# One layer's attention outputs turned and multiplied as they become ready, half of a conditioning vector computed later, and rows made by turning broadcast columns

## The chip, the cores and the metric

The program runs on 1 core of one Trainium2 chip. The metric is the device time in microseconds (us) of one execution. Each engine (PE the matrix engine, DVE, ACT, POOL, and SP, which issues most loads) works through its own list in order and meets the others at semaphores.

## The reference, cut to what matters

Two transformer blocks of depth 2 each, 256 positions of 1024 channels, all in f32. The change touches the first block:

```python
for layer in range(DEPTH):
    mod = c @ w_ada[layer] + b_ada[layer]
    sh_a, sc_a, g_a, sh_f, sc_f, g_f = [m[:, None, :] for m in jnp.split(mod, 6, -1)]
    h = x * (1.0 + sc_a) + sh_a
    u = h @ w_in[layer]
    ...
    mix = jnp.concatenate([y_ret, y_ssd, y_swa], -1) @ w_out[layer]
    x = _layer_norm(DEEPNORM_ALPHA * x + (1.0 + g_a) * mix, ln_g[layer, 0], ln_b[layer, 0])
    h = x * (1.0 + sc_f) + sh_f
    if layer % 2 == 0: f = _swiglu(h, ffn_w_gate[i], ffn_w_up[i], ffn_w_down[i])
    else:              f = _moe(h, router_w[i], router_b[i], ...)
    x = _layer_norm(DEEPNORM_ALPHA * x + (1.0 + g_f) * f, ln_g[layer, 1], ln_b[layer, 1])
```

`y_ret` (retention) has 256 columns, `y_ssd` 512 and `y_swa` (windowed attention) 256. The second block (mLSTM, convolution, cross-attention, FFN) is not touched.

## The kernel before, in words

**Weights.** Every weight matrix is streamed from HBM in chunks of 1 MB in the order of `stream_plan`. SP loads a chunk into a slot of RAW (two slots in the first mixer, four from the FFN on), ACT rounds it to HI (`split_hi`, line 430), DVE subtracts to get LO (`split_lo`, line 439), and PE makes each product from three matmuls (lines 444 to 446). A slot is free again after LO; HI and LO have three places each, free again when PE is done with the chunk.

**The conditioning vector.** `c @ w_ada` is not done on PE: DVE multiplies each 128-row piece of `w_ada` by a column of `c` and adds it to a sum (`ada_step`, lines 694 and 697), SP loads the pieces (`ada_load`, line 684), and at the end PE adds over the partitions with one-column matmuls (`pe_ada_sum`, line 725). The 12288 results of both layers are computed in blocks of 2048. In the first mixer, 32 pieces of 512 KB pass through two half slots of RAW: blocks 1 and 2 of layer 0. Block 2 holds the scale and the output gate (`g_f`) of the FFN. The 24 pieces of layer 1, 1 MB each, pass during the FFN (line 697 too), through two slots in AR.

**The end of a mixer** (`pe_mixer1`, `act_mixer1`, `dve_mixer1`, called for l = 0 and l = 1). DVE finishes retention (a norm over each head, lines 1453 to 1478), gates the SSD output in two halves (1467, 1470; each half waits for 8 or 16 matmuls of `y`, lines 1138 and 1140), and scales the attention output (1481). ACT squares the gated SSD output (1276), POOL takes the root, DVE applies it (1488). Then the 1024 mixed columns in R are turned (128x128 transposes on PE, line 544), rounded by ACT (572) and DVE (582, 584), and multiplied by the four chunks of `w_out` (c0 to c3 below): c0, c1, then c2 and c3 as a pair, bank by bank. All four chunks start only after all four turns have been issued. After each of the last pair's four banks DVE adds the residual and takes statistics (929, 931, 934), normalises (942), and PE turns X for the FFN or the router.

**Rows.** A vector that lies as columns (8 columns of 128) and is needed as a row in all partitions is made by DVE multiplying the identity by each column (`dve_diag`, line 894, 8 instructions) and PE multiplying ones by the result (`pe_rows`, line 901, 8 matmuls, two passes each). ACT copies it (907). This is done six times: (0,0), (0,1), (1,0), scale, shift and gate.

**What sets the order.** Everything is written out by hand. `sp_stream` issues chunk i, then the `ada_load`s that the table `SIDE_AFTER` or the FFN position names; each `ada_load` waits for the DVE step that frees its slot, and all later loads stand behind it on SP. `ada()` in `dve_mixer1` is a pair of `ada_step`s and stands between the `split_lo`s.

```python
SIDE_AFTER = {..., 13: (8,), 14: (9,), 15: (10, 11, 12), 16: (13, 14, 15)}
...
if i == (moe_first if l else CH["out0"][3] + 1):
    s.wait_ge(*dve_fm(("mix", l), "lo", 3))
    sp_gains(s, l, 0)
```

Chunks 13 to 16 are c0 to c3 of layer 0; 17 and 18 are the FFN's first gate and up chunks. In layer 1, after the last pair, PE multiplies early keys (`pe_keys`, line 1636), ACT issues eight small loads (`act_small`, lines 2275 and 2277) and copies the keys (1646), and only then PE turns X for the router (544).

## Time and profile before

| | |
|---|---|
| median of 3 runs | 2753.8 us (2753.72 to 2757.09) |
| the profiled execution, its span | 2756.4 us |
| PE busy in it | 2655.7 us (96%) |
| DVE busy in it | 2194.9 us (80%) |
| first mixer, FFN, second mixer end at about | 207, 429, 568 us |

The page names busy time of each engine, the granted clock of PE in 40 slices, the chain of waits that ended last and the costliest groups. Since PE is busy nearly all the time, what counts is where it is idle or at its lower clock: the timelines of single engines say that. One profiled execution is shown; it lies 2.6 us above the median.

### The profile page before, as it was taken

To read this page: it belongs to the slowest core of one execution; us is meant where nothing else is said; L and a number is where in the kernel's file an instruction comes from. 1 tells how busy PE (TensorE), PEld (TensorE's weight loads), DVE (VectorE), ACT (ScalarE), POOL (GpSimd) and SP (SyncE) were. 2 spreads that over 40 slices of the span, in tenths; PEclk is the share of its full clock that TensorE was granted. 3 is DMA by queue.
4 is the path that set the end of the run, shared out by engine and by line. 5 is a ranking of instruction groups with operands and counts; after the bars stand their busy time and mean duration, and the time that the engine had idled before them with its cause. 6 is when DMAs were issued, how large, how long until landed. Compare 5 with 4: busy or idle time off the path is not lost.

```text
span 2756.4 us, 37885 instructions
## 1 busy us (share of the span) xinstructions
PE 2655.7 (96%) x15712; PEld 2358.6 (86%) x15712; DVE 2194.9 (80%) x2513; ACT 1519.4 (55%) x1567; POOL 47.4 (2%) x83
## 2 busy tenths in 40 slices
PE   6969999989999999999999999999999999999998
PEld 5859998878888888888888889999899999998898
DVE  6967677778888888888888879885487788954777
ACT  3514335547677677777777754544554564444554
POOL 2000000000000000000000000000000000000000
PEclk9979999989999999999999999999999998999999
DMA  8649865369999999999999952354455533444453
GB/s 312 235 162 336 312 240 168 120 212 378 351 350 353 345 359 349 360 348 358 348 359 346 364 184 87 135 183 173 157 184 184 186 125 130 154 153 168 153 184 115
DMA packets 376065, 669.86 MB, mean 243 GB/s; under 512 B 26825, under 2 KB 199503, under 8 KB 371023
## 3 DMA queue, kind: packets, MB, share of 16 engines
q1 hardware_dynamic: 358400, 662.55, 68.2%
...
## 4 chain that ended last, share of the span: by engine, by line
PE 88%; DVE 7%; ACT 2%; DMA 1%; issue 1%; POOL 0%; ACTq 0%; SPq 0%; DVEq 0%; POOLq 0%
PE PS L444 25%; PE PS L446 24%; PE PS L445 24%; PE PS L544 2%; PE PS L2477 2%; DVE LO L439 2%; PE PS L1636 2%; DVE AR L2767 1%; PE PS L1871 1%; PE PS L1908 1%; PE PS L2363 1%; DMA RAW<-in_w_ada_dram 1%; ACT HI L430 1%; DVE AR L697 1%; PE PS L2354 1%
## 5 line engine op out<-in xcount | busy, mean ns | idle before, releaser
L439 DVE TENSOR_TENSOR LO<-RAW,HI 128x2048 fp32r<-128x2048 f32 x410 | 930.2, 2273 | 231.5 <-ACT HI L430 231.3
L430 ACT ACTIVATE HI<-RAW 128x2048 fp32r<-128x2048 f32 x410 | 780.0, 1903 | 346.3 <-PE PS L446 292.9
L444 PE MATMUL PS<-X1H,HI 128*128 128x256 f32 (+1 forms) x2128 | 611.4, 287 | 6.2 <-DVE X1L L584 4.2
L445 PE MATMUL PS<-X1L,HI 128*128 128x256 f32 (+1 forms) x2128 | 605.5, 285 | 0.0
L446 PE MATMUL PS<-X1H,LO 128*128 128x256 f32 (+1 forms) x2128 | 605.2, 284 | 0.0
L444 PE MATMUL PS<-HI,X1H 128*128 128x512 f32 x1056 | 431.6, 409 | 0.9 <-DVE LO L439 0.4
L444 PEld LDWEIGHTS PS<-X1H,HI 128*128 128x128 f32 (+1 forms) x2128 | 409.4, 192 | 11.1 <-issue 8.5
L446 PE MATMUL PS<-HI,X1L 128*128 128x512 f32 x1056 | 413.7, 392 | 0.0
L445 PE MATMUL PS<-LO,X1H 128*128 128x512 f32 x1056 | 413.0, 391 | 0.0
L445 PEld LDWEIGHTS PS<-X1L,HI 128*128 128x128 f32 (+1 forms) x2128 | 409.6, 192 | 2.0
L446 PEld LDWEIGHTS PS<-X1H,LO 128*128 128x128 f32 (+1 forms) x2128 | 409.3, 192 | 0.8
L439 DVE TENSOR_TENSOR LO<-AR,HI 128x2048 fp32r<-128x2048 f32 (+1 forms) x147 | 334.8, 2278 | 58.6 <-ACT HI L430 57.7
L430 ACT ACTIVATE HI<-AR 128x2048 fp32r<-128x2048 f32 (+1 forms) x147 | 280.2, 1907 | 121.3 <-PE PS L446 117.0
L444 PE MATMUL PS<-HI,X2H 128*128 128x512 f32 x840 | 333.9, 398 | 3.3 <-DVE LO L439 3.3
L445 PE MATMUL PS<-LO,X2H 128*128 128x512 f32 x840 | 330.8, 394 | 0.0
L446 PE MATMUL PS<-HI,X2L 128*128 128x512 f32 x840 | 330.5, 393 | 0.0
L444 PEld LDWEIGHTS PS<-HI,X1H 128*128 128x128 f32 x1056 | 199.2, 189 | 48.3 <-issue 8.5
L445 PEld LDWEIGHTS PS<-LO,X1H 128*128 128x128 f32 x1056 | 199.4, 189 | 45.5 <-issue 6.7
L446 PEld LDWEIGHTS PS<-HI,X1L 128*128 128x128 f32 x1056 | 198.8, 188 | 42.9
L2767 DVE SCALAR_TENSOR_TENSOR AR<-AR,PC 128x256 f32<-128x256 f32 x480 | 193.9, 477 | 0.1
L444 PEld LDWEIGHTS PS<-HI,X2H 128*128 128x128 f32 x840 | 160.4, 191 | 35.7 <-DVE LO L439 3.7
L446 PEld LDWEIGHTS PS<-HI,X2L 128*128 128x128 f32 x840 | 159.8, 190 | 34.1
...
## 6 DMA issues: line engine op xcount, KB each, us to landing
...
```

Source lines behind the costliest of these rows:

```text
L430: a.activation(HI[:, n % NH, 0:size(i)], raw_at(i), ACT.Copy).then_inc(*hi.up(i))
L439: v.tensor_tensor(LO[:, m % NH, 0:n], raw_at(i), HI[:, m % NH, 0:n].bitcast(F32), ALU.subtract).then_inc(*lo.up(i))
L444: t.matmul(o, lh, rh, start=first, stop=False)
L445: t.matmul(o, lh, rl, start=False, stop=False)
L446: return t.matmul(o, ll, rh, start=False, stop=last)
L544: z = t.transpose(d, s_, ident[0:n, 0:n])
L697: v.scalar_tensor_tensor(o, slot, pcol("c", k), o, ALU.mult, ALU.add).then_inc(*dve_ada.up("step", m))
L1636: z = t.matmul(PS[:, bank, 256 * nb:256 * nb + 256], w[:, c, 128 * nb:128 * nb + 128], cols[:, c, :], start=(c == 0), stop=(c == 7))
L1871: z = t.matmul(PS[:, gather_bank(x, half), 128 * c:128 * c + 128], HM[:, k, 512 * half + 128 * c:512 * half + 128 * c + 128], PP[:, x % 2, ...
L1908: t.matmul(PS[:, scatter_bank(x, q), :], PGT[:, x % 2, 128 * k:128 * k + 128], YE[:, x % 2, ns], start=True, stop=True).then_inc(*pe_moe.u ...
L2477: z = t.matmul(PS[:, b, 256 * k:256 * k + 256], MF[:, c, 128 * k:128 * k + 128], w[:, c, :], start=(c == 0), stop=(c == 7))
L2767: v.scalar_tensor_tensor(UC[:, c, :], UP[:, c, k:k + 256], pcol(f"cv_dw_w{l}", 8 * k + c), UC[:, c, :], ALU.mult, ALU.add).then_inc(*dve_t ...
```

## The change

1. **Mixed columns.** Their order in R becomes attention, retention, SSD, SSD, and the chunks of `w_out` are loaded in that order. PE turns the attention columns after the first half of `y`, the retention columns after the second, multiplies the first chunk, then turns the SSD columns, multiplies the second chunk and then the pair. ACT and DVE follow the same order; ACT squares each SSD half apart.
2. **Conditioning.** Block 2 of layer 0 keeps only its first 1024 results (8 pieces of 512 KB in place of 16). The other half, `g_f`, becomes sum 6: 4 more pieces of 1 MB (two row blocks of 1024 columns each) in the FFN, at the unit numbers n = 8, 17, 26 and 27 that had no piece. PE sums it right after sum 5.
3. **Rows.** `dve_diag` is gone. `pe_rows` turns each column, read 128 times over by a step of zero: 8 transposes.
4. **SP.** No `ada_load` stands behind c3 any more, two fewer stand ahead of it, and the two loads of gains move behind the FFN's first two chunks.

```diff
-        out += u_tm(A["w_out"][l], 0, 8, f"out{l}")
+        out += u_tm(A["w_out"][l], 6, 8, f"out{l}") + u_tm(A["w_out"][l], 0, 6, f"out{l}")
...
+    ADA, ADA_OF, ADA_SUM = [], {}, ((0, 0, 16), (0, 16, 16), (0, 32, 8), (1, 0, 16), (1, 16, 16), (1, 32, 16), (0, 40, 8))
+    STAGE = ([ar(8192 + 2048 * i, 2048) for i in range(4)], [RAW[:, 2, 0:1024], RAW[:, 2, 1024:2048]],
+             [ar(8192, 2048), ar(10240, 2048)])
+    SUMMED = (ar(2304, 2048), RAW[:, 3, :], RAW[:, 3, 0:1024], ar(12288, 2048), ar(14336, 2048), ar(12288, 2048),
+              ar(5120, 1024))
...
+        for k in range(8):
+            step(2, 1, ((k, 0, 1024),))
+        for n in (3, 4, 5):
             for k in range(8):
...
+                step(n, 2, ((k, 0, 2048),))
+            for k in ((0,), (2,), (4, 6))[n - 3]:
+                step(6, 2, ((k, 0, 1024), (k + 1, 0, 1024)))
...
-        for j in range(16):
-            z = t.matmul(PS[:, bank, j:j + 1], acc[:, 128 * j:128 * j + 128], ones[:, 0:1], start=True, stop=True)
+        for j in range(ADA_SUM[n][2]):
+            z = t.matmul(PS[:, bank, at + j:at + j + 1], SUMMED[n][:, 128 * j:128 * j + 128], ones[:, 0:1], start=True,
+                         stop=True)
...
-    DG = ar(5120, 8, 128)
-
-    def dve_diag(v, tag, cols):
-        for c in range(8):
-            z = v.tensor_scalar(DG[:, c, :], ident, cols[:, c:c + 1], None, ALU.mult)
-        z.then_inc(*dve_res.up("diag", tag))
-
-    def pe_rows(t, tag):
-        t.wait_ge(*dve_res("diag", tag))
+    def pe_rows(t, tag, cols, bank=0):
+
         for h in range(2):
-            for c in range(4):
-                z = t.matmul(PS[:, h, 128 * c:128 * c + 128], ones, DG[:, 4 * h + c, :], start=True, stop=True)
-            z.then_inc(*pe_res.up("rows", tag, h))
-
-    def act_rows(a, tag, dst):
+            turn(t, [(PS[:, bank + h, 128 * c:128 * c + 128], view(cols[:, 4 * h + c:4 * h + c + 1], [0, 128]))
+                     for c in range(4)]).then_inc(*pe_res.up("rows", tag, h))
+
+    def act_rows(a, tag, dst, bank=0):
         for h in range(2):
             a.wait_ge(*pe_res("rows", tag, h))
-            a.activation(dst[:, 512 * h:512 * h + 512], PS[:, h, :], ACT.Copy).then_inc(*act_res.up("rows", tag, h))
+            a.activation(dst[:, 512 * h:512 * h + 512], PS[:, bank + h, :], ACT.Copy).then_inc(*act_res.up("rows", tag, h))
...
-        t.wait_ge(*act_ev(f"in{l}r2", 1))
-        pe_rows(t, (l, 0))
-        t.wait_ge(*dve_mix("gate", l, 1))
-        for k in range(2):
+        def turn_mix(cp):
+            t.wait_ge(*dve_mix(("swa", "retout", "ssd", "ssd")[cp], l))
+            turn(t, [(PS[:, MIX_BANKS[cp], 256 * ci + 128 * tt:256 * ci + 128 * tt + 128],
+                      R[:, tt, 128 * (2 * cp + ci):128 * (2 * cp + ci) + 128])
+                     for ci in range(2) for tt in range(2)]).then_inc(*pe_fm.up(("mix", l), cp))
+
+        def y(k):
             for h in range(8):
                 xv = lambda j: XD[:, j, 64 * h:64 * h + 64]
                 o = PS[:, 4 + k, 64 * h:64 * h + 64]
...
                 if k:
                     z = t.matmul(o, E8[:, h, 256:384], xv(1), start=False, stop=True)
             z.then_inc(*pe_mix.up("y", l, k))
+
+        def out_rows(n):
+            i = CH[f"out{l}"][n]
+            t.wait_ge(*lo(i))
+            t.wait_ge(*dve_fm(("mix", l), "lo", n))
+            mm_down(t, i, lambda c: X2H[:, 2 * n + c, :], lambda c: X2L[:, 2 * n + c, :], [4, 5, 6, 7], n == 0,
+                    False).then_inc(*used.up(i))
+
+        t.wait_ge(*act_ev(f"in{l}r2", 1))
+        t.wait_ge(*dve_ada("mod", 4 if l else 1))
+        pe_rows(t, (l, 0), MOD[:, l, 16:24])
+        t.wait_ge(*dve_mix("gate", l, 1))
+        y(0)
+        turn_mix(0)
+        y(1)
+        turn_mix(1)
+        t.wait_ge(*dve_mix("gated", l, 1))
+        t.wait_ge(*act_mix("qt", l, 1))
+        out_rows(0)
         t.wait_ge(*act_res("rows", (l, 0), 1))
-        pe_to_fm(t, ("mix", l), R, [2, 3, 0, 1], order=MIXED,
-                 ready=lambda cp: dve_mix("retout", l) if cp == 0 else dve_mix("swa", l) if cp == 3 else dve_mix("ssd", l))
-        def between(j):
-            if l == 1 and j == 1:
-                t.wait_ge(*dve_fm(("mix", 1), "lo", 3))
-                pe_rows(t, "scale")
-            if l == 1 and j == 2:
-                t.wait_ge(*act_res("rows", "scale", 1))
-                pe_rows(t, "shift")
-            if l == 1 and j == 3:
-                t.wait_ge(*act_res("rows", "shift", 1))
-                pe_rows(t, "gate")
-
-        pe_gemm_tm(t, f"out{l}", X2H, X2L, [4, 5, 6, 7], lambda j: dve_fm(("mix", l), "lo", j), between)
-        if l == 0:
-            pe_ada_sum(t, 2, 1)
+        turn_mix(2)
+        turn_mix(3)
+        if l == 1:
+            t.wait_ge(*dve_fm(("mix", 1), "lo", 1))
+            t.wait_ge(*dve_res("combined", 1, 0))
+            pe_rows(t, "scale", HSC, 2)
+        out_rows(1)
+        if l == 1:
+            t.wait_ge(*dve_fm(("mix", 1), "lo", 3))
+            pe_rows(t, "shift", HSH)
+            t.wait_ge(*act_res("rows", "shift", 1))
+            t.wait_ge(*dve_ada("mod", 5))
+            pe_rows(t, "gate", MOD[:, 1, 40:48])
+        else:
+            pe_ada_sum(t, 2, 2)
+        pair = CH[f"out{l}"][2:]
+        for n in range(2):
+            t.wait_ge(*lo(pair[n]))
+            t.wait_ge(*dve_fm(("mix", l), "lo", 2 + n))
+        mm_down_pair(t, pair, lambda n, c: X2H[:, 4 + 2 * n + c, :], lambda n, c: X2L[:, 4 + 2 * n + c, :], [4, 5, 6, 7],
+                     f"out{l}").then_inc(*used.up(pair[1]))
...
-        for k in range(2):
+
+        def squares(k):
             a.wait_ge(*dve_mix("gated", l, k))
             for g in range(2):
                 z = a.activation(SQR[:, k, 256 * g:256 * g + 256], XS[:, k, 256 * g:256 * g + 256], ACT.Square,
                                  scale=1.0 / 16, accum_out=m4[:, 2 * k + g:2 * k + g + 1])
-        z.then_inc(*act_mix.up("ssdvar", l))
-        act_fm_scaled(a, ("mix", l), [2, 3, 0, 1], X2H, lambda c: pcol(f"ssd_norm{l}", c - 2) if 2 <= c < 6 else None, MIXED)
+            z.then_inc(*act_mix.up("ssdvar", l, k))
+
+        mixed = lambda *cps: act_fm_scaled(a, ("mix", l), MIX_BANKS, X2H, lambda c: pcol(f"ssd_norm{l}", c - 4) if c > 3 else None,
+                                           cps)
+        mixed(0)
+        squares(0)
+        mixed(1)
+        squares(1)
+        mixed(2, 3)
+        if l == 1:
+            act_rows(a, "scale", SCR, 2)
         split_hi(a)
         if l == 1:
-            act_rows(a, "scale", SCR)
             act_memory_cols(a, "router", 0, raw[slot_of[CH["mf"][0]]](CH["mf"][0]), raw_cols(CH["mf"][0]))
+            act_rows(a, "shift", SHR)
+            act_rows(a, "gate", GB2)
+        split_hi(a)
         split_hi(a)
         if l == 1:
-            act_rows(a, "shift", SHR)
-        split_hi(a)
-        if l == 1:
-            act_rows(a, "gate", GB2)
             act_small(a)
...
+        if l == 1:
+            dve_combine(v, 1, 0)
         gate(0)
         gate(1)
-        v.wait_ge(*pe_mix("pt", l, 3))
-        dve_diag(v, (l, 0), MOD[:, l, 16:24])
-        ada()
...
-        v.wait_ge(*dve_mix("skip", l))
-        for k in range(2):
+
+        def gated(k):
...
-        v.wait_ge(*act_mix("rg", l))
+
+        mixed = lambda *cps: dve_fm_scaled(v, ("mix", l), MIX_BANKS, X2H, X2L,
+                                           lambda c: pcol(f"ssd_norm{l}", c - 4) if c > 3 else None, cps)
         v.wait_ge(*pe_mix("pv", l))
         v.wait_ge(*dve_mix("den", l))
-        R4 = R[:, :, 768:1024].rearrange("p t (h d) -> p t h d", h=4)
+        v.tensor_tensor(R[:, :, 0:256].rearrange("p t (h d) -> p t h d", h=4),
+                        PS[:, 7, :].rearrange("p (t h d) -> p t h d", t=2, h=4), view(den, [4, 2], [1, 4], [0, 64]),
+                        ALU.mult).then_inc(*dve_mix.up("swa", l))
+        v.wait_ge(*dve_mix("skip", l))
+        gated(0)
+        v.wait_ge(*act_mix("rg", l))
         v.wait_ge(*pool_rs("ret", l))
         v.tensor_tensor(O8, O8, every8(v8), ALU.mult).then_inc(*dve_mix.up())
         v.wait_ge(*dve_mix.last())
-        v.tensor_tensor(R[:, :, 0:256], R[:, :, 768:1024], O8.rearrange("p (t h) d -> p t (h d)", t=2),
+        v.tensor_tensor(R[:, :, 256:512], R[:, :, 768:1024], O8.rearrange("p (t h) d -> p t (h d)", t=2),
                         ALU.mult).then_inc(*dve_mix.up("retout", l))
-        v.wait_ge(*dve_mix.last())
-        v.tensor_tensor(R4, PS[:, 7, :].rearrange("p (t h d) -> p t h d", t=2, h=4), view(den, [4, 2], [1, 4], [0, 64]),
-                        ALU.mult).then_inc(*dve_mix.up("swa", l))
-        if l == 0:
-            ada()
-        else:
-            split_lo(v)
+        mixed(0)
+        gated(1)
+        mixed(1)
+        split_lo(v)
+        v.wait_ge(*dve_mix("retout", l))
         v.wait_ge(*pool_rs("ssd", l))
-        v.tensor_tensor(R[:, :, 256:768].rearrange("p t (g d) -> p t g d", g=2),
+        v.tensor_tensor(R[:, :, 512:1024].rearrange("p t (g d) -> p t g d", g=2),
                         XS.rearrange("p t (g d) -> p t g d", g=2), view(m4, [2, 2], [1, 2], [0, 256]),
                         ALU.mult).then_inc(*dve_mix.up("ssd", l))
-        dve_fm_scaled(v, ("mix", l), [2, 3, 0, 1], X2H, X2L, lambda c: pcol(f"ssd_norm{l}", c - 2) if 2 <= c < 6 else None,
-                      MIXED)
-        if l == 1:
-            dve_combine(v, 1, 0)
-            v.wait_ge(*dve_res("combined", 1, 0))
-            dve_diag(v, "scale", HSC)
-        if l == 0:
-            split_lo(v)
         ada()
-        split_lo(v)
-        if l == 1:
-            v.wait_ge(*pe_res("rows", "scale", 1))
-            dve_diag(v, "shift", HSH)
+        mixed(2, 3)
+        split_lo(v)
         ada()
         split_lo(v)
-        if l == 1:
-            v.wait_ge(*pe_res("rows", "shift", 1))
-            dve_diag(v, "gate", MOD[:, 1, 40:48])
-        ada()
-        split_lo(v)
-        ada()
+        split_lo(v)
 
         def last_sum():
             if l == 0:
-                dve_ada_sum(v, 2, 1)
+                dve_ada_sum(v, 2, 2)
                 v.wait_ge(*dve_ada("mod", 2))
                 dve_combine(v, 0, 0)
...
             if n in (9, 18, 28):
                 t.wait_ge(*dve_ffn("ffn", "hid", p - 1))
                 pe_ada_sum(t, 2 + n // 9, 2 * ((p + 1) % 2))
+            if n == 28:
+                pe_ada_sum(t, 6, 2 * ((p + 1) % 2), 16)
...
-            t.wait_ge(*dve_ada("mod", 5))
+            t.wait_ge(*dve_ada("mod", 6))
...
-            pe_rows(t, (0, 1))
+            pe_rows(t, (0, 1), MOD[:, 0, 40:48])
...
-            if n < 27 and n not in (8, 17, 26):
-                ada_step(v, ada_of(n))
+            if n < 28:
+                ada_step(v, ADA1 + n)
...
+        dve_ada_sum(v, 6, 2, 16)
         dve_ada_sum(v, 5, 2)
-        dve_diag(v, (0, 1), MOD[:, 0, 40:48])
         dve_combine(v, 0, 1)
...
-            g.wait_ge(*act_mix("ssdvar", l))
+            g.wait_ge(*act_mix("ssdvar", l, 1))
...
     SIDE_AFTER = {1: (0,), 4: (1,), 5: (2,), 6: (3,), 8: (4,), 10: (5,), 11: (6,), 12: (7,), 13: (8,), 14: (9,),
-                  15: (10, 11, 12), 16: (13, 14, 15)}
+                  15: (10, 11)}
...
-                if i == (moe_first if l else CH["out0"][3] + 1):
+                if i == (moe_first if l else CH["out0"][3] + 3):
                     s.wait_ge(*dve_fm(("mix", l), "lo", 3))
                     sp_gains(s, l, 0)
...
-            if 0 <= n < 24 and n not in (8, 17):
-                ada_load(s, ada_of(n) + 2)
+            if 0 <= n < 26:
+                ada_load(s, ADA1 + n + 2)
```

On SP, behind c2 of layer 0 (first row), before:

```order
L419 DMA RAW<-in_w_out_dram 128x2x1024
L684 DMA RAW<-in_w_ada_dram 128x1024 x6
L419 DMA RAW<-in_w_out_dram 128x2x1024
L684 DMA RAW<-in_w_ada_dram 128x1024 x6
L916 DMA AR<-in_ln_g_dram 128x1024
L916 DMA AR<-in_ln_b_dram 128x1024
L419 DMA RAW<-in_ffn_w_gate_dram 128x8x256
```

and now:

```order
L419 DMA RAW<-in_w_out_dram 128x2x1024
L705 DMA RAW<-in_w_ada_dram 128x1024 x4
L419 DMA RAW<-in_w_out_dram 128x2x1024
L419 DMA RAW<-in_ffn_w_gate_dram 128x8x256
L419 DMA RAW<-in_ffn_w_up_dram 128x8x256
L933 DMA AR<-in_ln_g_dram 128x1024
L933 DMA AR<-in_ln_b_dram 128x1024
```

Ahead of c3 stand 4 pieces in place of 6, and none between c3 and the FFN's first chunk in place of 6 and the gains.

On DVE, layer 0, from the last turned SSD columns (line 584) to the residual (line 929, now 946), before:

```order
L584 SCALAR_TENSOR_TENSOR X2L<-PS,PC,X2H 128x256
L439 TENSOR_TENSOR LO<-RAW,HI 128x2048 [waits hi]
L697 SCALAR_TENSOR_TENSOR RAW<-RAW,PC 128x1024 [waits dve_ada,ada4]
L697 SCALAR_TENSOR_TENSOR RAW<-RAW,PC 128x1024 [waits dve_ada,ada5]
L439 TENSOR_TENSOR LO<-RAW,HI 128x2048 [waits hi]
L697 SCALAR_TENSOR_TENSOR RAW<-RAW,PC 128x1024 [waits dve_ada,ada4]
L697 SCALAR_TENSOR_TENSOR RAW<-RAW,PC 128x1024 [waits dve_ada,ada5]
L439 TENSOR_TENSOR LO<-RAW,HI 128x2048 [waits hi]
L697 SCALAR_TENSOR_TENSOR RAW<-RAW,PC 128x1024 [waits dve_ada,ada4]
L697 SCALAR_TENSOR_TENSOR RAW<-RAW,PC 128x1024 [waits dve_ada,ada5]
L439 TENSOR_TENSOR LO<-RAW,HI 128x2048 [waits hi]
L697 SCALAR_TENSOR_TENSOR RAW<-RAW,PC 128x1024 [waits dve_ada,ada4]
```

and now:

```order
L584 SCALAR_TENSOR_TENSOR X2L<-PS,PC,X2H 128x256
L439 TENSOR_TENSOR LO<-RAW,HI 128x2048 [waits hi]
L721 SCALAR_TENSOR_TENSOR RAW<-RAW,PC 128x1024 [waits dve_ada,ada4]
L721 SCALAR_TENSOR_TENSOR RAW<-RAW,PC 128x1024 [waits dve_ada,ada5]
L439 TENSOR_TENSOR LO<-RAW,HI 128x2048 [waits hi] x2
L946 TENSOR_TENSOR AR<-PS,AR 128x512 [waits pe_tm,act_res]
```

Four pairs of conditioning steps (the last row begins the fourth) stood between those columns and the residual; one is left. The LO of c1, once the first of four, now stands ahead of the SSD columns.

## Rows read from the trace of the kernel before

**Rows 1.** Page, part 1: busy us (share of the span) x instructions

```profile
PE 2655.7 (96%) x15712; PEld 2358.6 (86%) x15712; DVE 2194.9 (80%) x2513; ACT 1519.4 (55%) x1567; POOL 47.4 (2%) x83
```

**Rows 2.** Stretches: length, busy us (x) of five engines, PEclk, DMA share, GB/s

```profile
149.00:159.20 10.20, 7.01 (x24) 5.96 (x25) 9.38 (x15) 3.43 (x11) 1.44 (x2) 0.50 0.31 103
...
176.40:186.60 10.20, 8.19 (x36) 6.42 (x35) 0.00 (x0) 0.00 (x0) 0.00 (x0) 1.00 0.98 308
186.60:213.90 27.30, 12.90 (x58) 12.07 (x59) 21.52 (x36) 8.49 (x11) 1.62 (x4) 0.50 0.46 155
213.90:271.90 58.00, 56.88 (x432) 54.79 (x431) 45.09 (x27) 23.05 (x18) 0.00 (x0) 1.00 0.89 328
...
398.20:401.60 3.40, 3.40 (x19) 3.40 (x18) 2.97 (x15) 0.00 (x0) 0.00 (x0) 0.50 0.48 141
...
435.70:531.30 95.60, 92.43 (x645) 83.41 (x643) 73.71 (x132) 53.10 (x81) 2.72 (x5) 1.00 0.39 131
```

**Rows 3.** Chain of waits, 130 to 215 us: start, us, what

```profile
169.41 4.35 DMA RAW<-in_w_ada_dram
...
176.41 12.19 DMA RAW<-in_ffn_w_gate_dram
...
201.60 0.60 DVE AR L929
```

**Rows 4.** Timeline of SP: start, us from first to last issue

```profile
133.04 20.25 SPq L684 DMA_DIRECT2D RAW<-in_w_ada_dram  x6
160.11 0.38 SPq L419 DMA_DIRECT2D RAW<-in_w_out_dram  x1
161.30 14.12 SPq L684 DMA_DIRECT2D RAW<-in_w_ada_dram  x6
```

**Rows 5.** Timelines of DVE and ACT, first mixer's end [idle before <-releaser]

```profile
136.22 1.65 DVE L894 TENSOR_SCALAR AR<-CST,MOD 128x128 f32<-128x128 f32 x8
...
150.47 2.47 DVE L697 SCALAR_TENSOR_TENSOR RAW<-RAW,PC 128x1024 f32<-128x1024 f32 x2
```

```profile
165.04 1.92 ACT L430 ACTIVATE HI<-RAW 128x2048 fp32r<-128x2048 f32 x1 [8.06 <-DMA RAW<-in_w_out_dram]
```

**Rows 6.** Timeline of PE, first mixer's end and FFN start

```profile
138.02 3.04 PE L901 MATMUL PS<-AR,CST 128*128 128x128 f32 x16 [1.38 <-DVE AR L894]
...
149.97 1.94 PE L544 MATMUL PS<-CST,AR 128*128 128x128 f32 x8 [3.00 <-DVE AR L1478]
...
171.84 0.47 PE L444 MATMUL PS<-HI,X2H 128*128 128x512 f32 x1 [3.28 <-DVE LO L439]
...
211.79 0.56 PE L444 MATMUL PS<-X1H,HI 128*128 128x256 f32 x1
```

**Rows 7.** Chain of waits, 100 to 620 us: the FFN's end

```profile
394.16 3.47 PE PS L725 x32
...
410.44 0.87 PE PS L544 x8
411.32 1.79 PE PS L901 x16
```

**Rows 8.** DVE in the FFN: its timeline, then its conditioning steps grouped

```profile
390.45 2.29 DVE L439 TENSOR_TENSOR LO<-RAW,HI 128x2048 fp32r<-128x2048 f32 x1 [1.32 <-ACT HI L430]
392.66 0.68 DVE L1716 TENSOR_TENSOR AR<-AR,PS 128x512 f32<-128x512 f32 x1
```

```profile
L697 DVE SCALAR_TENSOR_TENSOR AR<-AR,PC 128x2048 f32<-128x2048 f32 x21 | 49.3, 2346 | 0.0
```

**Rows 9.** Timelines of ACT and PE, second mixer's end

```profile
564.86 0.40 ACTq L2275 DMA_DIRECT2D BT<-in_ml_w_gate_dram  x1
...
572.79 0.60 ACT L1646 ACTIVATE AR<-PS 128x512 f32<-128x512 f32 x1 [7.34 <-issue]
```

```profile
562.87 1.95 PE L901 MATMUL PS<-AR,CST 128*128 128x128 f32 x16
...
573.49 1.94 PE L544 MATMUL PS<-CST,X 128*128 128x128 f32 x16 [1.76 <-issue]
```

82 lines of the change are left out of this document (44 added, 38 removed).

## The prediction

> **What bounds the kernel now.** I read the page first. PE is busy 96% of the span and DVE 80% [rows 1], so time can only come out where PE is idle, runs at its lower clock, or does work that goes away. The second view is the granted clock by stretches [rows 2]: from 149.0 to 159.2 us and from 186.6 to 213.9 us it was 0.50 (1.2 GHz), in the long stretches 1.00 (2.4 GHz). The weak spot is the passage from the first mixer to the FFN. The stretch from 176.4 shows PE busy for 8.2 us, so the last pair of output products ended at 184.6; the FFN's first product started at 211.8 [rows 6]. These 27 us hold only a sum and the turns of X. The third view, the chain of waits, says what filled them [rows 3]: a conditioning piece under way for 4.35 us, then the FFN's first weight chunk for 12.2 us from 176.4, and DVE takes the last of the four banks of the residual at 201.6 although PE had finished it at 184.6. DVE's list has four conditioning pairs and the LO of that chunk ahead of the residual, and SP's list has the pieces ahead of the chunk.
>
> The same queue makes PE late earlier. SP spent 20.25 us on six pieces before c3 could be issued at 160.1, and 14.1 us on the six behind it [rows 4]; ACT got c3 at 165.0 [rows 5], and PE waited 3.3 us and started the pair at 171.8 [rows 6]. Before that PE waited 1.4 us for the diagonals and 3.0 us for the retention columns [rows 6]. Slices of a second kind stand at the second mixer's end [rows 9]: ACT issues eight small loads from 564.9 to 572.8, and PE, though done with the keys at 571.7, turns X only at 573.5.
>
> **The change, layer 0.** I lay the new order out with the durations of this trace.
> - Diagonals: DVE's 1.65 us at 136.2 goes [rows 5], as does the conditioning pair behind it (2.5 us and its wait). Retention, which began at 141.25, begins at 136.2. PE's rows cost 1.79 us as matmuls at the full clock [rows 7]; eight turns cost 0.87 us [rows 7]. The trace has no turn of a column read by a step of zero. Bounds: 0.87 us as any turn, 1.79 us if it went like the matmuls that it replaces. I take 0.87, the same instruction. PE had finished its previous work at 136.6 and goes on without the 1.4 us wait.
> - Rows 0.9, half of `y` 1.8, a turn, second half 3.6 us: `y` ends at 144.1 (was 147.0). DVE gates it (1.5 us after a short latency) by 145.8. c0, rounded at 132.5, then starts at 145.9 in place of 155.75 and takes 5.5 us, to 151.4. During it ACT squares, POOL takes the root (some 1.5 us) and DVE applies it by 150.2. The SSD turns and c1 follow to 157.8; c1's LO now comes at 148.7.
> - SP: the pieces behind c2 wait for the DVE pair that now runs from 150.2 to 152.7 (2.5 us [rows 5]). c3 goes out at 153.2, not 160.1 [rows 4]. It landed 4.9 us after its issue [rows 4, 5]; with a piece beside it I allow 5.4. HI 1.9 us [rows 5], then LO 2.3 us [rows 8] behind the last conditioning pair: ready at 163.0, against 171.6.
> - The sum over 8 columns of block 2, not 16, fits between 159.2 and 161.1, ahead of the pair. Three more conditioning pairs are no longer between PE and the residual. The FFN's first chunk leaves when c2's LO is done, at 156.7, lands at about 162.5, and its LO is done at 166.8, when the pair's first bank is done too. Nothing on DVE stands ahead of the residual after that.
> - The pair took 12.75 us (171.84 to 184.6) with a piece of slow clock; I keep that: 163.0 + 12.75 = 175.7. From the last bank to the FFN's first product it was 211.8 - 201.6 = 10.2 us [rows 3, 6]. New start: 185.9. **Term 1: 211.8 - 185.9 = -25.9 us.** Bounds: -22 if c0 falls to the low clock and c3 lands 2 us later; -29 if the pair runs at the full clock throughout (11.2 us) and the turns of X too.
>
> **The FFN.** It takes in 4 pieces of 1 MB, 4 steps of DVE (two halves of 1.28, so 2.5 us each) and 16 one-column passes on PE. The first two steps fall where DVE waits for HI; PE, busy 56.9 of the first 58.0 us [rows 2] and without a wait from there to unit 28, shows the cover; 21 grouped steps of DVE waited 0.0 us for data [rows 8], with the DMA engines at 0.89 in the first 58 us [rows 2]. I cost those at nothing; if that cover is gone, a step costs 2.5 us, or a chunk 2.8 us (328 GB/s at a share of 0.89 is 369 at full share). The last two fall at units 26 and 27. There DVE had one wait of 1.32 us [rows 8], then the hidden product at 392.66, and PE's sum started at 394.2 behind it. Adding 5.0 and taking off the wait moves that product to 396.3, and its end to 396.9: PE waits 2.8 us. Sum 6 is half of sum 5's 3.5 to 3.7 us [rows 7]: +1.8. Behind a sum the clock was 0.50 for 3.4 us [rows 2]; with 5 us more of little work I add one such stretch, 1.7 us lost. The rows (0,1) give back 0.9. The memory rows wait for the last step, now at about 396 in place of 387, and are needed at 408: free. **Term 2: +2.8 + 1.8 + 1.7 - 0.9 = +5.4 us** (bounds +1 and +10).
>
> **Layer 1.** There are no pieces here; DVE loses its four diagonals. `y` ends at 527.4 in place of 528.0, c0 starts at 529.1 in place of 536.6, because the SSD norm is no longer ahead of it. Then 5.5 for c0, 0.9 for two turns, 0.9 for scale, 5.5 for c1, 0.9 for shift, a new wait of some 1.6 us (gate goes to the banks that ACT must first have read, and ACT has 3.3 us of memory columns ahead of that), 0.9 for gate, 11.2 for the pair: its end is 556.5, against 562.9 [rows 9]. What counts is behind it: ACT's last HI waits for the pair's first chunk (about 555.0), ends at 556.9, and only then ACT issues its loads, 7.9 us (564.86 to 572.79 [rows 9]). The keys are copied at 565, PE turns X at 565.6 and not 573.5 [rows 9]. The new wait is hidden as long as it stays under 1 us more. **Term 3: -7.9 us** (bounds -6 and -9).
>
> Sum: -25.9 + 5.4 - 7.9 = **-28.4 us**, so a span of 2728.0 in place of 2756.4. That execution lay 2.6 us above the median of the three runs, which the sum leaves alone: **2725.4 us**.
>
> A rule that speaks against the change. Rows of turns here did not lower the clock: 435.7 to 531.3 is at 1.00 throughout [rows 2], and turns of four and eight in a row lie in it. The Trainium skill (TensorE: Matmul & The Clock Gate, Part 4: PE-mode transpose) says that the full clock does not engage for transposes, since they do not count as PE being busy in the same way. By that rule, the six sets of rows that were matmuls would each invite a stretch at 0.50; that is rival D.
>
> **The rivals.** All against 2753.8.
> - **A, the late chunk stays late.** c3 is still behind two pieces of conditioning, each waiting for a DVE step, and the FFN's second chunk behind c3's LO. If ACT, squaring in two parts between roundings, holds up the SSD norm by some 6 us and DMA is shared between c3, a piece and the FFN's chunk, the pair starts at 170 and the residual gains only the time after it. Half of term 1 is left, 13 us: -13 + 5.4 - 7.9 = -15.5, **2738**. For it: each load landed late wherever several were under way (12.2 us [rows 3]). Against: four such loads were, now two are.
> - **B, the FFN takes the extra pieces free.** DVE catches up before unit 26, and no further slow stretch comes: term 2 is +1, the sum -33, **2721**. For it: DVE's share in the FFN's later stretches is near 0.7. Against: units 26 and 27 come directly before the sum.
> - **C, the FFN becomes bound by SP and DMA: slower than before.** The gaps at n = 8 and 17 let the loads catch up; without them each unit needs two chunks of 1 MB, 5.7 us at 369 GB/s, and PE takes about 5.8 us for a unit (48 products 0.12 us apart). If each landing came 1.4 us late, 28 units would cost 39 us: -25.9 - 7.9 + 39 = +5, **2759**. It decides from 1.2 us a unit. Against: the DMA share was 0.89 [rows 2] and DVE never waited for a piece [rows 8] after the first.
> - **D, turns lower the clock.** Six sets of rows; a slow stretch of 3.4 us [rows 2] costs 1.7 us, and two in a row behind each would cost 3.4: +10 to +20, **2740**. Rows 2 speak against it.
> - **E, the change does nothing for the end of the mixer,** because something I don't see (the root on POOL, an order of semaphores) holds the residual: only terms 2 and 3, about -2, **2751**.
>
> **How the numbers follow.** Chances: forecast 0.63, A 0.13, B 0.11, C 0.03, D 0.06, E 0.04. The forecast's own range is 2719 to 2733 from the bounds. For 8 in 10 I go from 2715 (B with term 1 at its upper bound) to 2740 (A and D). A measurement of this kernel can tell 0.2%, 5.5 us, from no change. Faster by over 0.2%: the forecast, A, B and D, 0.93; within 0.2%: E, 0.04; slower: C, 0.03.
>
> **What would show it.** In the profile after: c0 of layer 0 starts near 146 and the pair near 163 us; SP issues c3 near 153; the FFN's first product starts near 186; no wait of PE for the FFN's first chunk. Sums 5 and 6 stand together near 371 with a PE wait of 2 to 3 us ahead. Rows take 0.9 us a set. In layer 1 the pair ends 26 to 27 us earlier than 562.9, counting terms 1 and 2, and X is turned 28 us earlier than 573.5; from there on both traces run in parallel. The forecast is wrong if the pair starts after 167, if the FFN from its first product to the last bank grows by over 10 us (it was 212), or if later parts differ by over 3 us.

## The result, and the profile after

| | before | after |
|---|---|---|
| median of all runs of this comparison | 2753.8 us (4 runs) | 2731.15 us (4 runs, 2726.36 to 2732.28) |
| ratio, 95% interval | | 0.9912 [0.9899, 0.9925] |
| the profiled execution, its span | 2756.4 us | 2730.0 us |
| PE's mean granted clock in it | 0.973 | 0.979 |

The changed kernel is faster by 0.9%. The median fell by 22.6 us where 28.4 were forecast; the spans of the two profiled executions lie 26.4 us apart. Two executions at a far lower clock, one of `cond_back2` (3769.6 us) and one of `both` (4887.9 us), are left out of every number below. The table of the three terms, read from the two traces:

| term | forecast | in the traces |
|---|---|---|
| 1, up to the FFN's first product | -25.9 | 211.79 to 189.90: -21.9 |
| 2, from there to the FFN's last bank | +5.4 | 212.3 to 218.0: +5.8 |
| 3, from there to the turning of X for the router | -7.9 | 149.4 to 139.2: -10.2 |
| sum | -28.4 | -26.4 |

From the router on both run in parallel: the spans differ by the 26.4 us that they differed by at the turning of X.

The page's busy line hardly moves against [rows 1]; PE is busy 12 us less, DVE 9:

```profile
PE 2643.8 (97%) x15664; PEld 2346.4 (86%) x15664; DVE 2186.1 (80%) x2466; ACT 1519.5 (56%) x1567; POOL 50.8 (2%) x83
```

**The first mixer's end.** The timeline of PE of the changed kernel, from the rows on (one line for each stretch that counts; start, busy us, what it did, and in brackets the idle time ahead and who ended it):

```profile
137.10 1.04 PE L544 MATMUL PS<-CST,MOD 128*128 128x128 f32 x8
137.98 1.90 PE L1158 MATMUL PS<-AR 128*128 128x64 f32 x16
140.28 0.66 PE L544 MATMUL PS<-CST,AR 128*128 128x128 f32 x4 [0.40 <-DVE AR L1527]
...
144.29 0.61 PE L544 MATMUL PS<-CST,AR 128*128 128x128 f32 x4
...
160.55 3.58 PE L749 MATMUL PS<-CST,RAW 128*128 128x1 f32 x16 [2.42 <-DVE RAW L721]
166.97 0.76 PE L444 MATMUL PS<-HI,X2H 128*128 128x512 f32 x1 [2.84 <-DVE LO L439]
...
188.07 2.18 PE L544 MATMUL PS<-CST,X 128*128 128x128 f32 x8 [1.75 <-DVE X1L L602]
189.90 0.56 PE L444 MATMUL PS<-X1H,HI 128*128 128x256 f32 x1
```

Of the two waits ahead of the rows and of the turned columns [rows 6] the first is gone and of the second 0.4 us are left, and a set of rows takes 1.04 us where the matmuls took 3.04 at the same place, mostly at the low clock (1.79 at the full one [rows 7]). c0 started at 146.03. PE then has nothing to do between c1 and the pair but the sum: it waits 2.4 and 2.8 us. The last line that answers to [rows 6] is the FFN's first product, at 189.90 for 211.79.

Why the pair starts at 167.0 and not at 163.0 stands in the timelines of SP and ACT and in the chain of waits of the same stretch:

```profile
133.17 21.16 SPq L705 DMA_DIRECT2D RAW<-in_w_ada_dram  x4
154.38 0.43 SPq L419 DMA_DIRECT2D RAW<-in_w_out_dram  x1
157.78 0.38 SPq L419 DMA_DIRECT2D RAW<-in_ffn_w_gate_dram  x1
```

```profile
162.47 1.91 ACT L430 ACTIVATE HI<-RAW 128x2048 fp32r<-128x2048 f32 x1 [8.64 <-DMA RAW<-in_w_out_dram]
165.26 1.91 ACT L430 ACTIVATE HI<-RAW 128x2048 fp32r<-128x2048 f32 x1 [0.88 <-DMA RAW<-in_ffn_w_gate_dram]
```

```profile
147.02 1.93 POOL SM L618
149.02 1.06 POOL SM L620
...
151.31 1.29 DVE RAW L721
152.70 1.29 DVE RAW L721
154.01 0.33 SPq L705
154.38 8.07 DMA RAW<-in_w_out_dram
162.47 1.92 ACT HI L430
164.42 2.30 DVE LO L439
```

The chain is the forecast's, link for link: POOL's root, the SSD norm on DVE, the conditioning pair, SP, c3. Two links were longer. POOL took 3.0 us for the root where I allowed 1.5, so SP issued c3 at 154.4, not 153.2; and c3, issued right behind the last two pieces, landed after 8.07 us, not 5.4.

Why the root took longer stands in the timelines of POOL and DVE. Its first operation in the kernel before, then DVE's LO of c1 in the changed kernel:

```profile
149.53 0.39 POOL L618 TENSOR_SCALAR SM<-SM 128x4 f32<-128x4 f32 x1 [2.91 <-ACT AR L1276]
```

```profile
146.56 2.28 DVE L439 TENSOR_TENSOR LO<-RAW,HI 128x2048 fp32r<-128x2048 f32 x1
```

In the changed kernel POOL's operation (147.02 in the chain) begins while that LO is under way and ends at 148.94, 0.1 us behind the LO's end at 148.84. So it is in both SSD norms of all fourteen traces of this case: the operation ends 0.1 us behind the DVE instruction that was under way when it began, be that a short product (0.39 us; before, `rows_only` and `order_back`), a conditioning step (1.06 us) or an LO (1.92 to 2.07 us). The new order has put c1's LO beside the root. No run moved it away, so what that would give is not shown.

c3 had company on both sides. The stretches from the last two pieces to c3's landing (columns as in [rows 2], the last is GB/s):

```profile
153.00:157.00 4.00, 4.00 (x19) 3.31 (x18) 4.00 (x6) 0.83 (x3) 0.00 (x0) 1.00 0.75 214
157.00:162.40 5.40, 2.98 (x15) 2.45 (x13) 3.23 (x3) 0.00 (x0) 0.00 (x0) 0.80 0.97 333
```

That is 2.65 MB, of which the two pieces and c3 are 2.1. The rest, by this estimate over half a megabyte, is the FFN's first chunk, issued at 157.78, 3.4 us behind c3: nothing else was issued on SP meanwhile.

**The FFN's end.** Timeline of PE, the one group of one-column matmuls (sums 5 and 6 together), and the stretch it lies in (columns as in [rows 2]):

```profile
372.08 10.40 PE L749 MATMUL PS<-CST,AR 128*128 128x1 f32 x48 [3.08 <-DVE AR L1756]
```

```profile
371.90:385.50 13.60, 13.42 (x63) 13.42 (x64) 4.18 (x11) 3.02 (x3) 0.00 (x0) 0.50 0.77 236
```

The wait of 3.1 us is the one forecast (2.8), from the hidden product behind DVE's two extra steps. But the 48 passes took 10.4 us where 5.3 were forecast, all of them at half clock, and the clock stayed low for 13.6 us, four times what follows sum 5 in [rows 2]. In return the stretches at the low clock at sums 3 and 4 were shorter in this execution (3.4 us each; 10.2 and 6.8 in that of before).

**The second mixer's end.** ACT's issues and the copy of the keys, then PE's keys and the turning of X, answering to [rows 9]:

```profile
538.18 1.92 ACT L430 ACTIVATE HI<-RAW 128x2048 fp32r<-128x2048 f32 x1 [5.88 <-PE PS L446]
538.20 0.40 ACTq L2315 DMA_DIRECT2D BT<-in_ml_w_gate_dram  x1
...
546.43 0.60 ACT L1684 ACTIVATE AR<-PS 128x512 f32<-128x512 f32 x1 [6.34 <-PE PS L1674]
```

```profile
539.28 7.07 PE L1674 MATMUL PS<-RAW 128*128 128x256 f32 x32
547.13 1.06 PE L544 MATMUL PS<-CST,X 128*128 128x128 f32 x8 [0.78 <-issue]
```

ACT's eight issues still fill 8 us, but they now begin together with the last HI and end when PE ends the keys. The copy waits for PE, not for the issues, and PE stands still for 0.78 us where it stood for 1.76 [rows 9]. The trace of before had shown that an issue need not wait for the activation ahead of it: its first one, at 564.86 [rows 9], stands beside this copy:

```profile
564.85 0.60 ACT L907 ACTIVATE AR<-PS 128x512 f32<-128x512 f32 x1 [0.30 <-PE PS L901]
```

### The profile page after: what moved, and what is told of

It is laid out like the page before. It is cut to its first block, busy times and chain, and to the rows that moved or that the text cites. A ratio compares the mean times of both kernels' runs of the same rounds, so it can differ in the third digit from the quotient of the medians.

```text
span 2730.0 us, 37737 instructions
## 1 busy us (share of the span) xinstructions
PE 2643.8 (97%) x15664; PEld 2346.4 (86%) x15664; DVE 2186.1 (80%) x2466; ACT 1519.5 (56%) x1567; POOL 50.8 (2%) x83
## 4 chain that ended last, share of the span: by engine, by line
PE 86%; DVE 8%; ACT 3%; issue 2%; DMA 1%; POOL 0%; ACTq 0%; DVEq 0%; POOLq 0%; SPq 0%
PE PS L444 24%; PE PS L446 24%; PE PS L445 24%; PE PS L544 2%; DVE LO L439 2%; DVE AR L721 2%; PE PS L2517 2%; PE PS L1674 2%; ACT HI L430 1%; DVE AR L2807 1%; PE PS L1911 1%; PE PS L1948 1%; PE PS L2403 1%; PE PS L2394 1%; PE PS L749 1%
```

## The experiments

Each ratio is against the kernel before on the same chip, over 4 to 11 runs of the kernel named; "-7.4 us" behind one is that share of 2754 us. Rows are of one execution each.

### The rows alone

```diff
-                z = t.matmul(PS[:, h, 128 * c:128 * c + 128], ones, DG[:, 4 * h + c, :], start=True, stop=True)
+            turn(t, [(PS[:, bank + h, 128 * c:128 * c + 128], view(cols[:, 4 * h + c:4 * h + c + 1], [0, 128]))
```

on the kernel before, `dve_diag` and its six calls removed.

> The kernel before with one part of the change: the six sets of rows made by turning. Theory 1 (a set saves its diagonals and half of PE's time, and turns leave the clock alone): layer 0 gains at most the 1.65 us of the diagonals on DVE, the FFN's end 0.9 us, layer 1 four sets of 1.0 us on PE between the chunks; together -4 to -7 us, and no stretch at the low clock that before does not have. Theory 2 (turns lower the clock): slow stretches behind the sets in layer 1, time 0 to +10 us.

Measured: ratio 0.9973 [0.9964, 0.9982], -7.4 us. Theory 1 holds, at its upper end or a little above it: FFN's first product at 210.64 (-1.2), and in layer 1, from the FFN's last bank to the turning of X, 146.8 for 149.4 us. It has one slow stretch of 10.2 us at the mixer's end in layer 1 where before has one of 6.8, in both at a wait of PE for the retention columns, and shorter ones in the FFN (the FFN took 207.2 us for 212.3, which is more than the 0.9 us of its one set); in sum turns cost no clock that the time would show.

### The conditioning undone, first try

```diff
+        for k in range(8):
+            for c0 in (0, 1024):
+                step(2, 1, ((k, c0, 1024),))
...
-                  15: (10, 11)}
+                  15: (10, 11, 12), 16: (13, 14, 15)}
```

on the changed kernel, with six `ada()` pairs at the mixer's end as before, and without sum 6.

> The changed kernel with its conditioning part undone: 16 pieces of block 2 and their six DVE pairs stand at the first mixer's end again, sum 6 is gone; mixed columns and rows stay as changed. Theory 1 (the mixer's end is held by the queue of pieces and pairs, so the new order alone cannot shorten it): FFN's first product near 208, hardly earlier than the 211.8 of before, FFN's end gains 1 us over before, layer 1 keeps its 10 us: about -14 us against before. Theory 2 (the new order of the mixed columns is what shortens layer 0): first product near 195, FFN not lengthened: about -28 us.

Measured: 0.9998 [0.9988, 1.0007], no gain at all, and FFN's first product only at 227. Neither theory: I had left PE's sum over block 2 ahead of the last pair, where the change has put it. The source view of the sum in this run:

```profile
L747 PE MATMUL PS<-CST,RAW x32: 352/352/372, 197.1 to 203.7; 128*128 128x1 f32 x32
its engine sat idle before it (us, times) until:
  DVE RAW L719: 27.8, 1
```

PE stood 27.8 us for the 16th piece with the pair's operands ready. The miss is of use: the change may put the sum ahead of the pair only because it has made the block small.

### The conditioning undone, the sum behind the pair

```diff
-        else:
-            pe_ada_sum(t, 2, 2)
         pair = CH[f"out{l}"][2:]
...
+        if l == 0:
+            pe_ada_sum(t, 2, 2)
```

> As cond_back, but PE's sum over block 2 stands behind the pair of chunks, where before has it: in cond_back the pair had to wait for it, and with it for all 16 pieces. Theory 1 (the queue of pieces holds the residual, so the new order of the mixed columns is worth nothing in layer 0 without the smaller block): pair at 169 to 171, FFN's first product at 206 to 209 against 211.8 in before, layer 1 keeps its 10 us: -13 to -16 us against before. Theory 2 (the new order shortens layer 0 by itself): first product near 200, -22 us.

Measured: 0.9954 [0.9938, 0.9969], -12.7 us. The FFN's first product stands at 210.85, less than 1 us before that of the kernel before, no earlier than with the turned rows alone (210.64) and later than even theory 1 had it; the second mixer's end keeps its 10.0 us. So with the old queue of pieces **the new order of the mixed columns is worth nothing in layer 0**. The queue of SP there shows it, beside [rows 4]:

```profile
131.68 24.98 SPq L703 DMA_DIRECT2D RAW<-in_w_ada_dram  x6
158.53 0.38 SPq L419 DMA_DIRECT2D RAW<-in_w_out_dram  x1
160.86 15.30 SPq L703 DMA_DIRECT2D RAW<-in_w_ada_dram  x6
```

c3, issued 1.9 us behind the sixth piece and 2.3 us ahead of the next, was 7.6 us under way.

### The order of the mixed columns undone

```diff
-        out += u_tm(A["w_out"][l], 6, 8, f"out{l}") + u_tm(A["w_out"][l], 0, 6, f"out{l}")
+        out += u_tm(A["w_out"][l], 0, 8, f"out{l}")
```

and the mixer's end of PE, ACT and DVE as before, with the smaller block and the turned rows kept.

> The changed kernel with the order of the mixed columns undone (c0 waits for all four sets of turned columns, old chunk order); conditioning and rows stay as changed. Theory 1 (in layer 0 the queue counts and the order only through SP's wait for the DVE step behind the SSD norm; in layer 1 the order is everything): layer 0 loses 2 to 4 us of its 21.9, layer 1 6 to 7 us of its 10.3: about -13 us against before. Theory 2 (the order matters in layer 0 as much as in layer 1): 6 us more are lost, about -7 us.

Measured: 0.9938 [0.9924, 0.9952], -17.1 us, 7 us less than the whole change. Theory 1 was right on layer 1 and still gave the order too much in layer 0. Timeline of SP, ACT and PE at the first mixer's end of this run:

```profile
157.83 0.38 SPq L419 DMA_DIRECT2D RAW<-in_w_out_dram  x1
```

```profile
162.67 1.92 ACT L430 ACTIVATE HI<-RAW 128x2048 fp32r<-128x2048 f32 x1 [7.97 <-DMA RAW<-in_w_out_dram]
```

```profile
167.16 0.47 PE L444 MATMUL PS<-HI,X2H 128*128 128x512 f32 x1 [1.93 <-DVE LO L439]
...
190.03 0.56 PE L444 MATMUL PS<-X1H,HI 128*128 128x256 f32 x1
```

c3 goes out 3.45 us later than in the changed kernel and is there 0.2 us later: 4.84 us under way, not 8.07. No piece is issued just ahead of it, and the FFN's first chunk only at 162.62. The first product is at 190.03 for 189.90. What the order gives in layer 0, an earlier issue of c3, the longer way of c3 takes away again. In layer 1, where no pieces are, the order gives 7.3 us (146.5 for 139.2 us from the FFN's last bank to the turning of X).

### c3 issued ahead of the last conditioning pair

```diff
-                  15: (10, 11)}
+                  15: (10,), 16: (11,)}
```

> The changed kernel with one number moved: SP issues c3 behind one pair of pieces and not two; DVE's list stays. Theory 1 (c3 was late, ready at 166.7, because SP waited for the DVE step of 151.3 to issue it): SP issues c3 at about 149, when c1's LO has freed its slot, it lands at 155 to 157, HI by 159; but its LO stands behind the last pair of conditioning, which now lands later, at about 162: pair from 164 to 165, about -2 us against the change. Theory 2 (DMA bandwidth, not the issue, sets the landing): c3 still lands near 162, the pair starts at 167, 0 us.

```profile
148.96 0.38 SPq L419 DMA_DIRECT2D RAW<-in_w_out_dram  x1
152.71 1.72 SPq L705 DMA_DIRECT2D RAW<-in_w_ada_dram  x2
```

```profile
153.89 1.92 ACT L430 ACTIVATE HI<-RAW 128x2048 fp32r<-128x2048 f32 x1
```

Theory 1: issued at 148.96, c3 had landed when ACT came to it at 153.9, within 4.9 us. Then DVE's list and the sum hold the pair, which starts at 163.75; first product 186.79, -3.1 us. The edit takes away both neighbours at once: the pieces are now issued behind c3, and the FFN's first chunk, again at 157.87, when c3 has landed. So this run alone does not say which of them made c3 late. That a load behind it costs little is what the kernel before suggests: there pieces were issued from 1.2 us behind c3 on, and c3 was used after 4.9 us [rows 4, 5]. The time: 2723.6 us, 0.9881 [0.9857, 0.9904], whose interval overlaps that of the change; the trace shows the 3 us, the times alone would not.

### The same, with c3's LO ahead of the last pair on DVE and the sum behind the pair on PE

```diff
         split_lo(v)
-        ada()
         split_lo(v)
+        ada()
         split_lo(v)
```

> As c3_sp, and DVE makes c3's LO ahead of the last conditioning pair, and PE sums block 2 behind the pair of chunks instead of ahead of it. Theory 1 (issue order holds c3): LO ready at 160 to 161, PE's pair starts at 161, the FFN's first product about 184 in place of 189.9, -6 us against the change. Theory 2 (bandwidth): 0 to -2 us. A third way: the sum, behind the pair at the low clock, holds up DVE's combination and X: -3 us.

PE's pair, and the sum behind it:

```profile
160.38 0.47 PE L444 MATMUL PS<-HI,X2H 128*128 128x512 f32 x1 [2.09 <-DVE LO L439]
...
171.37 1.84 PE L749 MATMUL PS<-CST,RAW 128*128 128x1 f32 x16
```

Pair at 160.4, first product at 183.77: -6.1 us, theory 1 to 0.3 us. The sum takes 1.84 us straight behind the pair and 3.58 between two waits. Of the 6.1 us the issue alone gave 3.1 (`c3_sp`); the rest came with the LO and the sum, which this run moves together. Time 2723.9 us, 0.9869 [0.9843, 0.9894], not to be told from `c3_sp`: of the 6.1 us, 4.5 are left at the FFN's last bank, because the slow stretches at sums 3 and 4 were 6.8 us each in this execution.

### Sum 6 apart from sum 5

```diff
-            if n == 28:
-                pe_ada_sum(t, 6, 2 * ((p + 1) % 2), 16)
+            if n == 29:
+                t.wait_ge(*dve_ada("mod", 5))
+                pe_ada_sum(t, 6, 2, 16)
```

and DVE's last step (n = 27) behind the hidden product.

> The changed kernel with DVE's last conditioning step (n = 27) behind the hidden product of the unit ahead, and PE's sum 6 one unit later, apart from sum 5. Theory 1 (PE's 3.1 us ahead of sum 5 are the two extra DVE steps ahead of the hidden product): the wait shrinks to about 0.5 us, -2.5 us against the change; sum 6 itself costs the same 3.5 us at the low clock or 1.8 at the full one. Theory 2 (the hidden product waits for ACT): the wait stays, 0 us, or the split sum brings a second slow stretch, +1.7 us.

```profile
369.13 3.74 PE L749 MATMUL PS<-CST,AR 128*128 128x1 f32 x32 [0.37 <-DVE AR L1757]
...
380.06 1.84 PE L749 MATMUL PS<-CST,AR 128*128 128x1 f32 x16
```

Theory 1 on the wait: 0.37 us for 3.08. But the gain in the trace is over three times the 2.5 us that it gave: the same 48 passes take 5.6 us for 10.4, the stretch at the low clock is 3.4 us for 13.6, and the FFN takes 209.5 us for 218.0. The one-column matmuls are the same in number; what is different is that they no longer stand together behind an idle PE. Which of the two counts, the wait or the standing together, this run does not separate. Time 2724.9 us, 0.9871 [0.9847, 0.9896], 6 us under the change by the medians, 11 by the ratios; in the profiled execution some of the 8.5 us is given back in slow stretches of the second mixer.

### Without sum 6

This kernel leaves out the product with `w_ada` in the FFN's output gate of layer 0, so it only prices the part.

```diff
-            for k in ((0,), (2,), (4, 6))[n - 3]:
-                step(6, 2, ((k, 0, 1024), (k + 1, 0, 1024)))
...
-        dve_ada_sum(v, 6, 2, 16)
+        v.tensor_scalar(MOD[:, 0, 40:48], pcols("b_ada0", 8, 40), 1.0, None, ALU.add).then_inc(*dve_ada.up("mod", 6))
```

> The changed kernel without sum 6 and its four pieces (the FFN's output gate of layer 0 is then its bias alone). Prices term 2. Theory 1 (the extra pieces cost only at units 26 to 28): the FFN from its first product to its last bank takes 210 to 212 us in place of 218, -6 to -7 us against the changed kernel, all of it from unit 26 on. Theory 2 (the pieces at units 8 and 17 cost too): the stretch up to unit 26 is shorter by over 1 us.

Measured: 0.9872 [0.9854, 0.9891], 10.5 us under the change; the FFN takes 209.5 us for 217.1 in `after_again` below. Up to sum 5 there is no difference but the wait: sum 5 starts 178.8 us behind the first product, and in the changed kernel PE runs out of products after 179.1 us and then waits 3.1. Theory 1: the pieces at units 8 and 17 were free. The cost of sum 6 as the change places it is 7.6 us in the trace; in both executions the slow stretches of the FFN add up to 21 to 22 us, so that is no luck of the clock. `sum6_late` took 209.5 us too with sum 6 in it, but its slow stretches add up to 11 us only. In `both` they are 20 us, and its FFN took 211.4: placed late, sum 6 costs about 2 us, which is its 16 passes (1.84 us). By the times `sum6_late` (0.9871) and this kernel (0.9872) are the same.

### The changed kernel again, and both improvements

> The changed kernel unaltered, as the yardstick of the other runs of this group: 22 to 25 us under before.

Measured: 2731.9 us, 0.9911 [0.9895, 0.9927]. The first measurement stands. In this second execution the pair starts at 167.68 and the FFN's first product at 190.80, 0.7 and 0.9 us later than in the first, so differences of under 1 us between two traces say nothing here.

> c3_first and sum6_late together. If the two gains lie in different stretches and add up: FFN's first product at 184, the FFN from there to its last bank 209 to 210 us in place of 218, together -12 us against the changed kernel. Rival: the low clock comes back elsewhere and takes a third of it: -8 us.

Measured: 2720.0 us, 0.9859 [0.9836, 0.9882]; 12 us under the change by the medians of this group, with intervals that don't touch. The two gains add up as forecast, in the times. In its profiled execution c0 fell into a slow stretch (142.8 to 153.1) and took 7.9 us for 5.75, so that the first product was at 187.7; the FFN took 211.4 us. It is faster than the kernel before and than the changed one; its interval overlaps those of `c3_sp`, `c3_first` and `sum6_late`.

### Sums that move more columns

On `both`; in the second run 128 columns, each result overwriting all but the first 24 columns of the one ahead.

```diff
-            z = t.matmul(PS[:, bank, at + j:at + j + 1], SUMMED[n][:, 128 * j:128 * j + 128], ones[:, 0:1], start=True,
-                         stop=True)
+            o, w = (24 * j, 128) if n > 2 else (at + j, 1)
+            z = t.matmul(PS[:, bank, o:o + w], SUMMED[n][:, 128 * j:128 * j + 128], ones[:, 0:w], start=True, stop=True)
```

> The kernel called both, and in the FFN's sums 3 to 6 each matmul moves 32 equal columns of ones in place of one (DVE then reads one column in 32). Theory 1 (a sum of one-column matmuls leaves PE with almost no columns moved, and the low clock follows that): the slow stretches of 3.4 to 6.8 us at the three sums shrink or go, the sums take no longer, -2 to -6 us against both. Theory 2 (the low clock follows the weight loads or an idle gap): the stretches stay, 0 us, or +1 us for the longer matmuls.

> As wide32 with 128 columns a matmul. Each pass then moves as many columns as a turn of 128 by 128, of which 16 took 1.9 us. Theory 1: no slow stretch at the sums of the FFN, a sum of 32 passes takes 3.6 to 4 us, -5 to -8 us against both. Theory 2: the stretches stay, and the sums take up to 0.5 us longer, 0 to +2 us.

Stretches at sums 3, 4 and 5, first of `both` (one column), then of the run with 128 columns:

```profile
248.60:255.40 6.80, 6.80 (x24) 5.83 (x24) 6.76 (x5) 0.11 (x1) 0.00 (x0) 0.50 0.84 308
306.70:313.50 6.80, 6.80 (x21) 5.74 (x22) 6.07 (x6) 0.65 (x2) 0.00 (x0) 0.50 1.01 366
371.50:374.90 3.40, 3.40 (x18) 3.40 (x18) 3.30 (x8) 0.14 (x1) 0.00 (x0) 0.50 0.58 155
```

```profile
243.30:247.10 3.80, 3.80 (x33) 3.80 (x34) 3.77 (x3) 2.40 (x2) 0.00 (x0) 1.00 1.07 382
302.80:306.60 3.80, 3.80 (x33) 3.80 (x34) 3.76 (x3) 2.40 (x2) 0.00 (x0) 1.00 1.09 400
365.00:368.80 3.80, 3.80 (x34) 3.80 (x35) 3.15 (x4) 2.98 (x3) 0.00 (x0) 1.00 0.03 8
```

With 128 columns the sums ran at the full clock (2.4 GHz), 3.8 us each, and no slow stretch followed any of them; the only one left between 200 us and the FFN's last bank (256.8 to 260.2) lies at a wait of PE of 3.0 us for DVE. With 32 columns nothing changed: 6.8, 3.4 and 6.8 us. So what theory 1 forecast for the clock came in the run with 128 columns and not in the one with 32, as far as one profiled execution of each shows. Little of it reached the time: the FFN took 210.5 us for the 211.4 of `both`, because PE now waited those 3.0 us for DVE, which `both` does not. The times show no gain: 2716.3 us (0.9867 [0.9848, 0.9886]) for 128 columns, 2721.2 (0.9871) for 32, against 0.9859 for `both`, and the intervals overlap.

## Why the prediction was right, and where it wasn't

The sign, the size and the place of each term held; the forecast was 5.7 us too fast, inside its range. The terms were 2.0 us too fast in sum (-28.4 for -26.4). The other 3.7 us are a slip of mine: I set the span of the profiled execution against the median time, but the time of an execution is 1.8 us more than its span (2731.76 and 2730.0 us), so by an estimate from these two numbers that of before lay 4.4 us above its median and not 2.6; that of after lay 0.6 above its own.

What each part gave, from the ratios, each good to 2.5 to 4.3 us: rows 7.4 us, order with rows 12.7 (so order about 5), smaller block with rows 17.1 (so block about 10), all three 24. In sum the parts give 22 to 23: as far as that can be told they hardly need each other. The block's 10 are a difference: against `rows_only`, `order_back` gains 20.6 us up to the FFN's first product and loses 11.4 in the FFN.

- **Term 1 (-25.9 forecast, -21.9).** The early steps held to 0.1 us: c0 at 146.03 (145.9). The step that failed is "c3 goes out at 153.2 ... with a piece beside it I allow 5.4": SP issued it 1.2 us later, because POOL's root stood beside c1's LO on DVE, and it landed after 8.07 us, 2.7 us more than I allowed, right behind two pieces and with the FFN's chunk behind it. The pair (12.81 us) and the way from the last bank to the first product (10.1) were as forecast. `c3_sp` shows the price of that place in the queue: issued ahead of the pieces, the chunk took under 5 us, and with nothing else moved the pair started at 163.75, 3.2 us earlier. Whether the pieces ahead or the chunk behind weighed more is not separated. This is rival A's mechanism (a late c3 behind two pieces, DMA shared with the FFN's chunk), at a third of its price. My sign of being wrong, a pair that starts after 167, was missed by 0.03 us here (166.97) and met in `after_again` (167.68).
- **The credit within term 1.** I gave the earlier c0 a place in the sum. `order_back` shows that it was worth under 1 us (its first product is at 190.03, for 189.90 and 190.80 in the two executions of the changed kernel), and `cond_back2` beside `rows_only` that without the smaller block it was worth nothing. Of the 21.9 us the rows gave 1.2; the rest is the queue's: fewer pieces ahead of c3, none between c3 and the FFN's first chunk, one pair in place of four ahead of the residual. The forecast of the time was nearly right with a step in it that did nothing.
- **Term 2 (+5.4, +5.8).** The wait of PE (3.1 for 2.8 us) and the rows (1.91 for 2.95 us with the late parameters) were as forecast, and the first extra pieces were free. The step that was mis-sized is "one more slow stretch, 1.7 us lost": the stretch at sums 5 and 6 was 13.6 us long where sum 5 alone had 3.4, 10.2 us more at half the clock, so 5 us lost. Against `no_sum6`, whose own stretch is 6.8, sum 6 costs 7.6 us, where my steps gave it 6.3. The difference to before hides it, because in that execution the stretches at sums 3 and 4 were 10.2 and 6.8 us, in that of after 3.4 and 3.4: 5 us given back, and 1 us lost again at the first products, of which more ran at the low clock.
- **Term 3 (-7.9, -10.2).** Counted from the FFN's last bank, the pair ended 7.5 us earlier than before where I had 6.4 (the slow stretch of before at c0, 531.3 to 538.2, has no counterpart). The step that failed is "only then ACT issues its loads": the issues began at 538.20, together with the last HI at 538.18, not 1.9 us behind it, and so no longer held PE. That the order is what counts here is shown by `order_back` (7.3 us of the 10.2).
- **Rival D (turns lower the clock).** From 419.7 to 552.8 us, with four sets of turned rows in it, the changed kernel is at 1.00 throughout:

```profile
419.70:552.80 133.10, 127.53 (x827) 112.90 (x826) 102.98 (x163) 73.02 (x116) 6.95 (x9) 1.00 0.47 141
```

and `rows_only` is faster by 0.27%. The rule of the Trainium skill (TensorE: Matmul & The Clock Gate, Part 4: PE-mode transpose), that the full clock does not engage for turns, would have brought slow stretches there; sets of eight to sixteen turns between matmuls did not, and eight turns themselves took 1.04 us there, and 2.18 us in a stretch at 0.50 (188.07 above). In this the trace differs from the Trainium skill. Turns are not cleared altogether: in `sum6_late`, `both` and `wide32` a slow stretch of 3.4 us stands at c0 of layer 1, behind two sets of four turns and a wait of 1.1 us; the other eight traces with this order have none there. How a long row of turns alone would fare no run here shows.

What stays open: why the slow stretches at one and the same sum are 3.4 us in one execution and 6.8 in another. Single executions of one kernel differ by 9 us (2713.6 to 2722.2 for `both`) and by 16 (2711.3 to 2727.2 for `wide32`), more than most of the steps above; how much of that the stretches are is not shown. Pieces ahead of c3 and a chunk behind it were not tried apart either.
